# Expert weights of a mixture-of-experts layer fetched in transfers of three units in place of two

## The reference

```python
g_sel = argmax(hf @ w_rg)                     # one of 8 groups of experts
e_top = top_k(softmax(e_logits[g_sel]), 2)    # two of its 8 experts
gate = p_group * p_top / sum(p_top)
y[token] += gate * (silu(x @ w_gate[e]) * (x @ w_up[e])) @ w_down[e]
```

## Time and profile before

| | us |
|---|---|
| median of 3 runs (2228.77 to 2234.33) | 2228.98 |
| the profiled execution | 2234.28 |
| its span | 2232.5 |
| TensorE busy | 1918.1 (86%) |
| DMA queue of SyncE | 584.31 MB, 63.6% of 16 engines' span |

### The profile page before, as it was taken

How to read it: one execution, slowest core, us unless ns; L and a number is a source line. 1 busy time by engine, 2 the same in 40 slices (tenths; PEclk the granted TensorE clock), 3 DMA queues, 4 the chain that set the end, 5 groups by cost and what they waited for, 6 DMA issues and landing times. The chain is left out here.

```text
span 2232.5 us, 24285 instructions
## 1 busy us (share of the span) xinstructions
PE 1918.1 (86%) x10222; PEld 1161.4 (52%) x10222; DVE 945.0 (42%) x1509; ACT 372.3 (17%) x751; POOL 0.2 (0%) x4
## 2 busy tenths in 40 slices
PE   8999886667766767766677999999999999999998
PEld 5687743333323333322233787784446787874445
DVE  7858321121111212212223264487752254577762
ACT  1123200000000000000001222122333222123332
POOL 0000000000000000000000000000000000000000
PEclk9999998888888888988888999999999999999999
DMA  7223699999999999999997334445532433336330
GB/s 306 76 76 124 278 411 431 431 431 432 430 430 431 430 431 432 426 431 432 432 431 314 117 151 170 132 148 195 207 118 109 151 151 140 139 110 252 151 151 20
DMA packets 31927, 594.78 MB, mean 266 GB/s; under 512 B 3918, under 2 KB 5200, under 8 KB 7512
## 3 DMA queue, kind: packets, MB, share of 16 engines
q1 hardware_dynamic: 29912, 584.31, 63.6%
q10 hardware_dynamic: 1920, 9.09, 1.3%
HBM read 590.22 MB, written 1.06 MB: 265 GB/s over the span
## 5 line engine op out<-in xcount | busy, mean ns | idle before, releaser
L1998 PE MATMUL ps<-ring,arena 128*32 128x512 f32 x2032 | 293.4, 731 | 150.7 <-DMA ring<-in_w_experts 142.5
L612 PE MATMUL ps<-arena,ring 128*128 128x256 f32 x1792 | 399.9, 379 | 1.0 <-DVE arena L1163 0.8
L612 PEld LDWEIGHTS ps<-arena,ring 128*128 128x128 f32 x1792 | 334.2, 189 | 49.5 <-issue 3.4
L806 PE MATMUL ps<-ring,arena 128*128 128x512 f32 x656 | 286.4, 593 | 0.0
L1998 PEld LDWEIGHTS ps<-ring,arena 128*32 128x32 f32 x2032 | 74.3, 130 | 352.6 <-issue 224.9
L806 PEld LDWEIGHTS ps<-ring,arena 128*128 128x128 f32 x656 | 124.7, 190 | 154.9 <-issue 154.7
L2028 PE MATMUL ps<-ring,arena 128*32 128x256 f32 x2016 | 152.3, 454 | 60.8 <-DMA ring<-in_w_experts 60.1
L2642 DVE COPY arena<-ps 128x256 f32<-128x256 f32 x64 | 27.2, 425 | 271.9 <-PE ps L2028 271.9
L2028 PEld LDWEIGHTS ps<-ring,arena 128*32 128x32 f32 x2016 | 71.5, 128 | 128.8 <-issue 80.6
L1954 PE MATMUL ps<-arena 128*128 128x256 f32 x256 | 78.3, 431 | 34.9 <-DVE arena L2642 34.9
L2632 DVE TENSOR_TENSOR arena<-arena,ps 128x512 f32<-128x512 f32 x16 | 11.0, 690 | 229.8 <-PE ps L1998 229.8
(11 more groups left out here) (439 smaller groups left out, 2072.7 us busy)
## 6 DMA issues: line engine op xcount, KB each, us to landing
ring<-in_w_experts SPq DMA_DIRECT2D x90, 4096.0 KB, 23.4
ring<-in_w_layers SPq DMA_DIRECT2D x64, 2048.0 KB, 7.8
ring<-in_w_experts SPq DMA_DIRECT2D x10, 2048.0 KB, 8.0
ring<-in_w_first SPq DMA_DIRECT2D x9, 2048.0 KB, 7.6
early<-in_w_layers SPq DMA_DIRECT2D x6, 2048.0 KB, 8.4
arena<-in_w_mem SPq DMA_DIRECT2D x4, 2048.0 KB, 18.1
ring<-in_w_first SPq DMA_DIRECT2D x4, 512.0 KB, 6.8
early<-in_w_experts SPq DMA_DIRECT2D x1, 2048.0 KB, 26.2
```

The source lines that it names most:

```text
L612: last = pe.matmul(ps[:, j % 2, 0:SEQ], t[:, s, k, :], lhs[:, k, :], start=(k == 0), stop=(k == KD - 1))
L806: last = pe.matmul(ps[:, bank, :], lhs[:, k, :], rhs[:, k, :], start=(first and k == 0), stop=(k == n - 1), skip_group_check=True)
L1998: last = pe.matmul(ps[CAP * e:CAP * (e + 1), v // 4, :], xg[:, (v % 4) * 2 + k, CAP * e:CAP * (e + 1)], w[:, k, e, :], start=(v % 4 == 0 a ...
```

## The change

Transfers carry three units: the array in HBM has 64 blocks of three units instead of 96 of two, so that a partition's row of a transfer is 48 KB instead of 32 KB. The ring then has two halves of three slots, and unit v sits in slot v%6. A transfer waits until all three units of its half are done. TensorE waits for three units at a time.

The last group is taken out of the loops of SyncE and TensorE. Units 0 to 8 are still three transfers, 9 and 10 are one each, and 11 is two of half a unit; TensorE does the first half of unit 11 before it waits for the second. The units of the layers go to slots 0, 1, 2, after units 6, 7, 8. The register that held the number of rounds now holds the number of further rounds.

```diff
-SLOT2 = (2, 0, 1)
+SLOT2 = (0, 1, 2)
-            def expert_pair(v, g, free):
-                s = (v + 2) % RING
-                sp.wait_ge(sem("unit_free"), free + v + 2)
-                src = d["w_experts"][bass.ds(g * 6 + v // 2, 1), :, :].rearrange("a p n -> (a p) n")
-                sp.dma_start(ring[:, s:s + 2, :].rearrange("p a n -> p (a n)"), src).then_inc(sem(f"w2_in{s}"), 16)
+            def expert_three(v, g, free):
+                s = v % RING
+                sp.wait_ge(sem("unit_free"), free + v + 3)
+                src = d["w_experts"][bass.ds(g * 4 + v // 3, 1), :, :].rearrange("a p n -> (a p) n")
+                sp.dma_start(ring[:, s:s + 3, :].rearrange("p a n -> p (a n)"), src).then_inc(sem(f"w2_in{s}"), 16)
...
-                for v in range(0, 12, 2):
-                    expert_pair(v, g, g * 12 + (g == 1 and v < 4))
+                for v in range(0, 12, 3):
+                    expert_three(v, g, g * 12 - (g == 1 and v < 6))
...
+            with sp.Fori(NH + 2, more_rounds * NGRP + NGRP - 1) as it:
+                g = sp.snap(it % NGRP)
+                for v in range(0, 12, 3):
+                    expert_three(v, g, it * 12)
+            last_group = sp.snap(more_rounds * NGRP + NGRP - 1)
+            for v in range(0, 9, 3):
+                expert_three(v, NGRP - 1, last_group * 12)
+            for v in range(9, 12):
+                s = v % RING
+                half = v % 3 * WSLOT
+                rows = d["w_experts"][(NGRP - 1) * 4 + v // 3]
+                sp.wait_ge(sem("unit_free"), last_group * 12 + v + 1)
+                if v < 11:
+                    sp.dma_start(ring[:, s, :], rows[:, half:half + WSLOT]).then_inc(sem("tail10" if v == 10 else f"w2_in{s}"), 16)
+                else:
+                    for i in range(2):
+                        at = i * WSLOT // 2
+                        sp.dma_start(ring[:, s, at:at + WSLOT // 2], rows[:, half + at:half + at + WSLOT // 2]).then_inc(sem(f"tail11_{i}"), 16)
             for u in range(RING2):
-                sp.wait_ge(sem("unit_free"), n_rounds * (NGRP * 12) + (SLOT2[u] - 2) % RING + 1)
+                sp.wait_ge(sem("unit_free"), more_rounds * (NGRP * 12) + NGRP * 12 + SLOT2[u] + 1)
...
-                    pe.wait_ge(sem(f"w2_in{s // 2 * 2}"), it * 32 + (v // RING + 1) * 16)
+                    pe.wait_ge(sem(f"w2_in{s // 3 * 3}"), it * 32 + (v // RING + 1) * 16)
...
+                        if tail and v == 11 and c == 2:
+                            pe.wait_ge(sem("tail11_1"), 16)
```

More of the change, by code:

```diff
@@ L1609, in _ @@
                 if u == 2:
-                    sp.dma_start(early[:, :], d["w_experts"][5][:, WSLOT:2 * WSLOT]).then_inc(sem("early_in"), 16)
+                    sp.dma_start(early[:, :], d["w_experts"][3][:, 2 * WSLOT:3 * WSLOT]).then_inc(sem("early_in"), 16)
                 if u == 1:
@@ L1616, in _ @@
                     sp.dma_start(four, d["fourier"]).then_inc(sem("in_four"), 16)
-            def expert_pair(v, g, free):
-                s = (v + 2) % RING
-                sp.wait_ge(sem("unit_free"), free + v + 2)
-                src = d["w_experts"][bass.ds(g * 6 + v // 2, 1), :, :].rearrange("a p n -> (a p) n")
-                sp.dma_start(ring[:, s:s + 2, :].rearrange("p a n -> p (a n)"), src).then_inc(sem(f"w2_in{s}"), 16)
+            def expert_three(v, g, free):
[3 more added lines that the diff above has]
+                sp.dma_start(ring[:, s:s + 3, :].rearrange("p a n -> p (a n)"), src).then_inc(sem(f"w2_in{s}"), 16)
             def unit_rows(v):
-                return d["w_experts"][v // 2][:, v % 2 * WSLOT:(v % 2 + 1) * WSLOT]
+                return d["w_experts"][v // 3][:, v % 3 * WSLOT:(v % 3 + 1) * WSLOT]
             def first_unit(v):
@@ L1665, in _ @@
             sp.wait_ge(sem("rounds"), 1)
-            n_rounds = sp.value_load(rounds[0:1, 0:1], min_val=1, max_val=SEQ // CAP)
-            with sp.Fori(NH + 2, n_rounds * NGRP) as it:
+            more_rounds = sp.value_load(rounds[0:1, 0:1], min_val=0, max_val=SEQ // CAP - 1)
+            with sp.Fori(NH + 2, more_rounds * NGRP + NGRP - 1) as it:
                 g = sp.snap(it % NGRP)
-                for v in range(0, 12, 2):
-                    expert_pair(v, g, it * 12)
+                for v in range(0, 12, 3):
[14 more added lines that the diff above has]
+                        sp.dma_start(ring[:, s, at:at + WSLOT // 2], rows[:, half + at:half + at + WSLOT // 2]).then_inc(sem(f"tail11_{i}"), 16)
             for u in range(RING2):
-                sp.wait_ge(sem("unit_free"), n_rounds * (NGRP * 12) + (SLOT2[u] - 2) % RING + 1)
+                sp.wait_ge(sem("unit_free"), more_rounds * (NGRP * 12) + NGRP * 12 + SLOT2[u] + 1)
                 layer_unit(sp, u)
@@ L1956, in scatter, with expert_weights @@
                 last.then_inc(sem("scatter_ps"), 1)
-            def expert_weights(it, v, first):
-                s = FIRST_SLOT.get(v) if first else (v + 2) % RING
-                if not first:
-                    pe.wait_ge(sem(f"w2_in{s // 2 * 2}"), it * 32 + (v // RING + 1) * 16)
+            def expert_weights(it, v, first, tail):
+                s = FIRST_SLOT.get(v) if first else v % RING
+                if tail and v >= 10:
+                    pe.wait_ge(sem("tail10" if v == 10 else "tail11_0"), 16)
+                elif not first:
+                    pe.wait_ge(sem(f"w2_in{s // 3 * 3}"), it * 32 + (v // RING + 1) * 16)
                 elif v == 3:
@@ L1972, in expert_weights, with expert_group @@
                 return ring[:, s, :]
-            def expert_group(it, mem_job=None):
+            def expert_group(it, mem_job=None, tail=False):
                 if mem_job == 0:
@@ L1994, in expert_group @@
                         pe.wait_ge(sem("xg"), 2 * it + 1 + v // 2)
-                    w = expert_weights(it, v, mem_job == 0).rearrange("p (k e n) -> p k e n", k=2, n=FE)
+                    w = expert_weights(it, v, mem_job == 0, tail).rearrange("p (k e n) -> p k e n", k=2, n=FE)
                     for k in range(2):
@@ L2023, in expert_group @@
                         scatter(it, v - 9)
-                    w = expert_weights(it, v, mem_job == 0).rearrange("p (c e n) -> p c e n", c=4, n=SEQ)
+                    w = expert_weights(it, v, mem_job == 0, tail).rearrange("p (c e n) -> p c e n", c=4, n=SEQ)
                     q = v - 8
                     for c in range(4):
+                        if tail and v == 11 and c == 2:
+                            pe.wait_ge(sem("tail11_1"), 16)
                         for e in range(GRP):
@@ L2035, in _ @@
             pe.wait_ge(sem("rounds"), 1)
-            n_rounds = pe.value_load(rounds[0:1, 0:1], min_val=1, max_val=SEQ // CAP)
-            with pe.Fori(PEELED, n_rounds * NGRP) as it:
+            more_rounds = pe.value_load(rounds[0:1, 0:1], min_val=0, max_val=SEQ // CAP - 1)
+            with pe.Fori(PEELED, more_rounds * NGRP + NGRP - 1) as it:
                 expert_group(it)
+            expert_group(pe.snap(more_rounds * NGRP + NGRP - 1), tail=True)
         @block.scalar
@@ L2221, in _ @@
             act.wait_ge(sem("rounds"), 1)
-            n_rounds = act.value_load(rounds[0:1, 0:1], min_val=1, max_val=SEQ // CAP)
-            with act.Fori(PEELED, n_rounds * NGRP) as it:
+            more_rounds = act.value_load(rounds[0:1, 0:1], min_val=0, max_val=SEQ // CAP - 1)
+            with act.Fori(PEELED, more_rounds * NGRP + NGRP) as it:
                 expert_group(it)
@@ L2604, in _ @@
             link(dve.tensor_scalar(first[:, 0, :], first[:, 0, :], 1.0 / CAP, 0.5 - 0.5 / CAP, ALU.mult, ALU.add))
-            link(dve.tensor_scalar(first[:, 0, :], first[:, 0, :], MAGIC, -MAGIC, ALU.add, ALU.add))
+            link(dve.tensor_scalar(first[:, 0, :], first[:, 0, :], MAGIC, -MAGIC - 1.0, ALU.add, ALU.add))
             dve.tensor_copy(rounds[:, 0:1], first[:, 0, :]).then_inc(sem("rounds"), 1)
             dve.wait_ge(sem("rounds"), 1)
-            n_rounds = dve.value_load(rounds[0:1, 0:1], min_val=1, max_val=SEQ // CAP)
+            more_rounds = dve.value_load(rounds[0:1, 0:1], min_val=0, max_val=SEQ // CAP - 1)
             mc = Chain(dve, sem("expert_chain"))
             per = 4
-            with dve.Fori(0, n_rounds) as r:
+            with dve.Fori(0, more_rounds + 1) as r:
                 with dve.Fori(0, NGRP) as g:
@@ L2695, in expert_units @@
     out[:, 8:] = np.asarray(down).reshape(NGRP, GRP, 4, P, 4, SEQ).transpose(0, 4, 3, 2, 1, 5).reshape(NGRP, 4, P, WSLOT)
-    return out.reshape(NGRP * 6, 2, P, WSLOT).transpose(0, 2, 1, 3).reshape(NGRP * 6, P, 2 * WSLOT)
+    return out.reshape(NGRP * 4, 3, P, WSLOT).transpose(0, 2, 1, 3).reshape(NGRP * 4, P, 3 * WSLOT)
 def layout(a):
```

## The result

| | before | changed |
|---|---|---|
| median (runs) | 2229.57 (4) | 2267.88 (4; 2264.6 to 2275.99) |
| the profiled execution | 2234.28 | 2264.6 |
| its span | 2232.5 | 2262.8 |
| ratio, 95% interval | 1 | 1.017 [1.0155, 1.0185] |

The change makes the kernel 38 us slower by the medians. The prediction had 2240.7 (2246 on the profiled execution) with a range of 2223 to 2256: the direction was right, the size about three times too small, and the time lies outside the range. The two profiled executions are 30.3 us apart, and it is these 30 us that the traces can account for: before, the slowest of four runs was profiled, after the change the fastest.

A forecast was written before the change was run, and what follows sets the result against it. The prediction took the expert stage to be bound by its weight bytes at 430 GB/s. Its terms, +12.5 +2 +1 -2.5 +4 -5.3, gave +11.7 us: 2246 on the profiled execution, 2240.7 on the median, range 2223 to 2256.

The forecast's parts named there:

- tail: After the last expert landing: only half of unit 11 is left, 1.0 us instead of 6.8; -5.3 us.
- Its own sign of being wrong: Expert stage: landings keep their 14.5 us beat through the long jobs, or miss it in groups without a job as well.
- long jobs: Groups 4, 5, 10, 11: 512-column job after unit 3 releases units 3 to 5 3.1 to 3.2 us too late; +12.5 us.
- short jobs: Groups 1 to 3, 6 to 9: 256-column job puts the release of units 3 to 5 on the limit; +2 us (0 to 9).
- releases of units 6 to 8 and 0 to 2: All 15 groups: units 6 to 8 released 11.25 us after landing, together +1 us (0 to 6); units 0 to 2 7.3, no loss.
- releases of units 9 to 11: End of each group: released 9.3 us after landing, or 11 with a cold start; no loss.
- hold-ups: Expert stage: instruction fetches delay single DMA engines, and more count when the queue is nearly empty; +4 us (-5 to +25).
- bytes: Expert transfers: 48 KB rows need a third fewer packets, each costing about 0.01 us beside its bytes; -2.5 us.
- the rest: First issue of group 1, SyncE's waits and registers, TensorE leaving its loop: 0 us.
- The limit of R: R, landing until TensorE releases that half, may reach 12.2 us (11.7 to 13.6): 14.57 less a fixed part of 2.4.
- rival C: Expert transfers: rows of 48 KB are cut, +10 us on top of the forecast, 2251; chance 0.05.
- B: Expert stage: starvation everywhere, limit 11.7, units 6 to 8 late in all groups; +33 us, 2262; chance 0.08.

## Why the prediction was wrong

The mechanism was right in the main: the prediction named the late release and the missing slack. Two places were missing: units 9 to 11, which it put at nothing, and the tail. Its own sign of being wrong came true as well: the landings also miss their beat in groups without a job, by 5.0 us together before units 3 to 5 of groups 13 to 15 (a part of the last one is a hold-up). The terms of the sum, against the profiled executions:

| term | predicted | measured |
|---|---|---|
| long jobs | +12.5 | +16.5 |
| short jobs | +2 | +11.1 |
| releases of units 6 to 8 and 0 to 2 | +1 | +4.4 |
| releases of units 9 to 11 | 0 | +12.4 |
| hold-ups | +4 | in the rows above (some 6); -6.9 that were there before |
| bytes | -2.5 | -2.8 |
| tail | -5.3 | -0.3 |
| the rest | 0 | -4.1 |
| sum | +11.7 | +30.3 |

**The limit of R.** The step that failed first is the fixed part, taken as 2.4 us from one 2048 KB transfer. The late transfers themselves show more. These are the issues at 532.35, 595.95, 906.81 and 969.58:

```profile
ring<-in_w_experts SPq DMA_DIRECT2D x1, 6144.0 KB, 19.1
ring<-in_w_experts SPq DMA_DIRECT2D x1, 6144.0 KB, 18.1
ring<-in_w_experts SPq DMA_DIRECT2D x1, 6144.0 KB, 17.6
ring<-in_w_experts SPq DMA_DIRECT2D x1, 6144.0 KB, 19.0
```

They need 3.1 to 4.6 us more than their bytes. The limit was thus near 10 to 11.4 us and not 12.2. R itself was well estimated for the jobs: 15.4 for the long ones (14.3 to 15.5 measured), 12.0 for the short ones (10.9 to 12.1). For units 6 to 8 it was too high (11.25; 7.8 to 10.8 measured), for units 0 to 2 too low (7.3; 5.5 to 11.4). Because the short jobs sat exactly at the limit, a limit lower by 1 to 2 us became 9 us in the sum. A term that lies on its threshold should have had its error carried through all its seven occurrences; I had written "0 to 9" and then used 2.

**Units 9 to 11.** The prediction gave them R = 9.3, or 11 cold, and no loss. It let only unit 9 run cold. In ten of fourteen groups that is what happens, R is 10.6 to 11.3, and the 11 of the prediction was right; these ten lose 5.3 us, 2 of them to the hold-up in the last group. In the other four (3, 4, 9 and 14, counted by the transfer that comes late) R is 12.7 to 13.5, and they lose 7.1 us. There the clock stays low through unit 9 and the scatter and into unit 10: in group 13 all three units take 13.1 us in place of 10.5 in group 14 (mean clock 0.65 and 0.84 in the windows above). That each piece of work behind a wait starts cold was in the prediction, for units 3 to 8. For units 9 to 11 it was left out because today's rows show short pauses there; the change makes those pauses longer, 2.9 and 3.5 us in the two groups shown, against 1.21. In which groups unit 10 is cold too does not go by the length of the pause: it is not behind pauses of 9.0 and 9.5 us (groups 5 and 4), but it is behind one of 4.8 (group 8). Why is not shown.

**The tail.** The prediction asked whether unit 10 was out of the way when unit 11 landed, and did not ask where TensorE stood. Units 6 to 8 land together, 14.7 us before the last byte, and from there TensorE needs 6.5 us for units 6 and 7, 2.15 for the activation and about 12.6 for four units and the scatters between them: 21.2 us. The experiments that split units 6 to 8 too, with threes and with pairs, took 5.4 and 5.7 us off it, where the sum had promised 5.3.

**Hold-ups.** The prediction feared that an emptier queue would make more of them count. With the queue never dry they sum to the same 7.0 us. In the changed kernel the single engines tell part of them from the late releases: the fifteenth engine of the four transfers above had landed 17.5 to 17.9 us after the issue, 3.0 to 3.3 above the bytes. The last one adds 0.2 us in the second and the third, but 1.6 and 1.3 in the first and the fourth, and there it is a hold-up. Without hold-ups the limit would be near 11.2 to 11.6. So the four long jobs lost 13.6 us by their lateness, near the predicted 12.5, and 2.9 to two fetches.

**The bytes** came out: 0.05 us for each transfer of three. The working had a slip: 89.4% of 16 x 22 us over 496 packets are 0.634 us and not 0.6146. The right size is in the packets themselves, which take 0.611 us with 16 KB, 1.213 with 32 KB and 1.815 with 48 KB, so that a packet costs 0.009 us beside its bytes. A 48 KB row goes as one packet, so rival C is out.

Of the rivals, B (starvation everywhere, 2262) was the nearest, with a chance of 0.08. Its condition, a limit at 11.7 or below, is the one that held. That its total came so near is in part luck: it had +15 for hold-ups and the full gain of the tail, which did not come, and nothing for units 9 to 11. The remaining 8 us between 30 and 38 are differences between executions of which there is no trace.

## What to carry to other kernels

Here a ring with three transfers outstanding forgave the long jobs and the cold clock, and one with two did not. Count the depth of a ring in transfers that can be outstanding, not in bytes, before trading it for size. With two halves, write down for each half the longest time from landing to release, in the clock that the new pauses will give, and put work that needs no new weights into the wait and not behind it. For a tail, follow the consumer back to the last point at which it was waiting, and cut the transfers from there on.

## What the runs showed of the hardware that was not expected

The stage can be run at a mean granted clock of 0.99 (nearly all of it at 2.4 GHz) instead of 0.86 by extra matmuls in its waits (clock of the window 302 to 1180), and the whole kernel is then at 1.0002. It is not free at the end: in the last group such matmuls stood before units that had landed, and without them the time from the last landing to the layers fell from 11.8 to 6.6 us. What a clock of 0.99 would give the kernel before, where no release is late, no run shows.

A transfer that finds the queue empty is not like one in a row. The issue at 969.58 needed 16.4 us until the first of the 16 engines had raised the semaphore, and 19.0 until the last had; the one at 906.81 needed 16.4 and 17.6. In all four late transfers the first engine comes 1.9 to 2.0 us above the bytes. The trace has the parts: the first packet starts 0.95 us after the issue, the first packet of an engine takes 1.8 to 3.4 us where later ones take 1.815, and the last engine's semaphore follows its last packet by 0.3 to 0.5 us. The Trainium skill, "DMA: Bandwidth & Descriptors", section on the anatomy of one DMA, puts the fixed cost at about 2.0 us for transfers that GpSimd issues. SyncE issues these. The first engine agrees with the figure here, the last one, which decides, does not (3.1 to 4.6).
